# Reversed order within an attention step of a hybrid decoder layer on eight cores: value product, transposes, normalisation, then the scores of the newest unit

## The reference, cut to what matters

```python
s = jnp.einsum('nqkgd,nskd->nkgqs', q, k) * ATTN_SCALE      # 16 query heads, 4 key heads
s = jnp.where(mask, s, NEG)                                 # band of 128 keys
m = jnp.maximum(jnp.max(s, axis=-1, keepdims=True), sk)     # sk: the sink logit of the head
e = jnp.exp(s - m)
den = jnp.sum(e, axis=-1, keepdims=True) + jnp.exp(sk - m)
p = (e / den).astype(v.dtype)
o = jnp.einsum('nkgqs,nskd->nqkgd', p, v)
```

## Time and profile before

| | |
|---|---|
| three runs | 3579.36, 3603.8, 4138.53 us; median 3603.8 |
| the profiled execution | 3581.02 us |
| span of its slowest core, which the profile shows | 3579.5 us |
| spans of the eight cores | 3561.9 to 3579.5 us |
| mean granted TensorE clock of that core | 0.979 |
| busy: PE, DVE, ACT, POOL | 96%, 30%, 24%, 13% of the span |

### The profile page before, as it was taken

The page is one execution under the profiler, slowest core; times in us unless marked ns, Lnnn a source line. Parts: engine busy times, 40 slices in busy tenths (PEclk is TensorE's granted clock), DMA queues, the critical chain, the costliest instruction groups (busy, mean ns, idle before and its releaser), DMA issues.

```text
span 3579.5 us, 62299 instructions; the slowest of 8 cores (3561.9 to 3579.5 us)
## 1 busy us (share of the span) xinstructions
PE 3422.9 (96%) x24208; PEld 2206.9 (62%) x24208; DVE 1076.8 (30%) x2012; ACT 846.2 (24%) x1925; POOL 478.4 (13%) x604
## 2 busy tenths in 40 slices
PE   7979999999999989999999999998879999999997
PEld 5546777777776545666666666664546666666664
DVE  2424222222234435122222222345442222222223
ACT  2444122111101444113210201013441132110103
POOL 0112021011012113003000100121130030000003
PEclk9989999999999999999999999999989999999998
DMA  8774686677678373556555555676665676665663
GB/s 171 120 144 99 132 168 119 126 144 150 141 163 185 78 143 79 125 112 139 110 121 131 122 126 116 135 145 145 133 146 114 124 147 121 128 121 104 115 114 93
DMA packets 83264, 460.62 MB, mean 129 GB/s; under 512 B 7552, under 2 KB 39936, under 8 KB 61568
## 3 DMA queue, kind: packets, MB, share of 16 engines
q0 software_dynamic: 27520, 351.48, 53.0%
q1 hardware_dynamic: 55456, 105.17, 10.2%
HBM read 784.43 MB, written 31.49 MB: 228 GB/s over the span
## 4 chain that ended last, share of the span: by engine, by line
PE 86%; DVE 4%; DMA 4%; ACT 3%; issue 2%; POOL 1%; SPq 0%; DVEq 0%; ACTq 0%; POOLq 0%
PE ps L130 86%; DVE R L130 2%; DMA AT<-wdb 2%; ACT AT L130 1%; DVE TMP L130 1%; DMA yT<-R 1%; ACT TMP L130 1%; DMA MIX<-xm 1%; POOL R L130 1%; DVE sm L130 0%; ACT R L130 0%; DVE AT L130 0%; ACT ring L130 0%; SPq L130 0%; ACT GT L130 0%
## 5 line engine op out<-in xcount | busy, mean ns | idle before, releaser
L130 PE MATMUL ps<-N,w 128*128 128x384 bf16 (+3 forms) x11712 | 1796.1, 315 | 0.0
L130 PEld LDWEIGHTS ps<-N,w 128*128 128x128 bf16 x11712 | 1143.4, 98 | 643.5 <-issue 40.8
L130 PE MATMUL ps<-MIX,w 128*128 128x320 bf16 (+2 forms) x4608 | 688.8, 313 | 0.0
L130 PEld LDWEIGHTS ps<-MIX,w 128*128 128x128 bf16 x4608 | 450.9, 98 | 236.5
L130 PE MATMUL ps<-GT,w 128*128 128x320 bf16 (+2 forms) x3072 | 459.4, 313 | 0.0
L130 DVE SCALAR_TENSOR_TENSOR ring<-ps,TMP 128x320 f32<-128x320 f32 (+2 forms) x384 | 201.1, 524 | 678.6 <-PE ps L130 675.6
L130 DVE TENSOR_TENSOR R<-ps,R 128x320 f32<-128x320 f32 (+2 forms) x384 | 201.5, 525 | 676.4 <-PE ps L130 676.4
L130 PEld LDWEIGHTS ps<-GT,w 128*128 128x128 bf16 x3072 | 300.6, 98 | 157.9 <-issue 0.2
L130 PE MATMUL ps<-R,w 128*128 128x320 bf16 (+2 forms) x1536 | 247.4, 324 | 23.1 <-DVE R L130 11.9
L130 POOL TENSOR_TENSOR TMP<-TMP 128x320 f32<-128x320 f32 (+2 forms) x222 | 209.4, 947 | 432.9 <-ACT TMP L130 432.9
L130 ACT ACTIVATE TMP<-R 128x320 f32<-128x320 f32 (+2 forms) x288 | 138.7, 490 | 403.8 <-DVE R L130 394.0
(11 more groups left out here) (107 smaller groups left out, 1442.4 us busy)
## 6 DMA issues: line engine op xcount, KB each, us to landing
w<-w_up POOLq DMA_DIRECT2D x48, 2048.0 KB, 15.1
w<-w_dn POOLq DMA_DIRECT2D x48, 2048.0 KB, 14.4
w<-w_in POOLq DMA_DIRECT2D x45, 2048.0 KB, 14.3
w<-w_ac POOLq DMA_DIRECT2D x12, 2048.0 KB, 15.4
w<-w_out POOLq DMA_DIRECT2D x12, 2048.0 KB, 14.3
AT<-xm SPq DMA_DIRECT2D x32, 384.0 KB, 8.6
AT<-xm SPq DMA_DIRECT2D x32, 352.0 KB, 7.0
MIX<-uscr SPq DMA_DIRECT2D x52, 167.0 KB, 6.1
```

Of the source, the lines that this page charges most:

```text
L130: ins = getattr(engobj, fn[0])(*fn[1], **fn[2])
```

## The change

The loop over the steps runs the same four parts in the opposite order. Nothing else differs: the same instructions on the same units, banks and tiles.

```diff
             for k in range(n + 4):
                 if G.SA and k in (2, 9):
                     make_qc(k > 2)
+                if 0 <= k - 4 < n:
+                    units[k - 4].V()
+                if 0 <= k - 3 < n:
+                    units[k - 3].Tr()
+                if 0 <= k - 1 < n:
+                    units[k - 1].N()
                 if k < n:
                     units[k].S()
-                if 0 <= k - 1 < n:
-                    units[k - 1].N()
-                if 0 <= k - 3 < n:
-                    units[k - 3].Tr()
-                if 0 <= k - 4 < n:
-                    units[k - 4].V()
                 yield
```

## The result

The changed kernel is slower: ratio 1.0335 to the kernel before, 95% interval 1.0238 to 1.0433. Its two runs that count took 3714.59 us, the profiled one, and 3703.33 us; runs in which a whole die had a lower granted clock, which come with either kernel, are left out throughout. The ratio is taken to the mean of three runs of the kernel before (3579.36, 3582.6 and 3603.8 us). The forecast was 3690 us, in 3630 to 3745.

What follows compares the result with a forecast made beforehand. The prediction took a 4.84 us ring through ACT and DVE, near TensorE's 4.36 us, to bound attention steps. Its terms made 418.6 us against 313.7, +105 us on 3581, stated as 3690 us, range 3630 to 3745.

Steps and rivals of the forecast that it cites:

- The ring through GpSimd: 60 attention steps: GpSimd's sink copy waits behind the previous unit's multiply; 6.31 us a step without tanh, 7.73 with.
- V and Tr on DVE: 24 tanh steps: the reciprocal waits behind the dense group's product and Tr's masking, making a step 7.73 us.
- the masking: DVE's masking of Tr ahead of the reciprocal in the 24 tanh steps, 0.57 us each.
- the output of V: Tanh stages: each fourth step DVE brings V's result out ahead of the masking, 0.57 us, 3.4 us in all.
- The sum: All 60 attention steps: 227.2 + 185.5 + 5.9 = 418.6 us against 313.7 us before, +105 us.
- the parts that were named and left out: Table load in each group's first step and added mask in group 1 lengthen a ring; some 6 us, not counted.
- the last step of each group is partly caught by the emptying steps: Each attention group's last step, 3 us, partly overlaps four emptying steps; not counted, 9 us in the lower bound.
- The clock: TensorE's clock drop in attention, 1.38 us: hidden under a 6.31 us ring, up to 2.2 us over in 12 steps.
- The rival that had the clock in the attention cost 40 us: TensorE's clock stays low in the attention, making TensorE the bound: +40 us, time 3726 us, chance 0.13.
- Mostly hidden: Attention steps: TensorE already sets them at 5.23 us, so the longer ring costs +30 us, 3611 us; chance 0.13.
- faster: Attention: V's bank emptied earlier and transposes ahead of the scores remove TensorE's waits; at best 3529 us, chance 0.02.

## Why the prediction was right

**The ring through GpSimd.** Right, and shown. It was worked out as 6.31 us and 7.73 us a step; the trace has 6.32 in `q_stage`, 6.39 in `ua_stage` and 7.77 in the plain tanh steps of group 2. N moved alone gives 105.4 us, taking most sink copies away takes 94 us back, and a second multiply lengthens these steps by the 1.18 us that it adds. There are 61 waits of 2.1 us on average where 60 of 1 to 3 us were forecast. One sentence on the rows is loose, without effect on the sum: only a start on another engine lies 0.1 us behind the end before it. On the same engine the next start comes before that end (the tanh at 1227.40, with the last read of a sum ending at 1227.50). The links were taken from start to start, so they hold.

**V and Tr on DVE.** Right in kind, a little high in size. A plain tanh step of group 2 takes 7.77 us in the changed order and 7.18 us with N alone, which is the masking, worked out as 0.57 us. Over all steps the two kernels differ by 13.6 us (432.7 and 419.1), where 13.7 us for the masking and 3.4 us for the output of V were worked out. By themselves, ahead of S but with N behind it, V and Tr cost 9.4 us in the steps by the medians and give 3 us back at the sample units.

**The sum.** Somewhat low: 418.6 us, measured 432.7. The 36 steps without tanh took 236.2 us where 227.2 were worked out, and the 24 with tanh 196.5 where it was 191.4. Half of the 14 us are the parts that were named and left out: the load of ACT's table takes 1.28 us in the first step of each group, and the added mask 0.8 us in four steps of group 1, together 7.0 us. The rest is in the 6.39 us of `ua_stage`, taken as 6.31, and in the tanh stages of groups 1 and 3, where steps with more dense groups or with the output of V reach 8 us and more; these I had counted too few.

**From the sum to the time.** +105 us stood for 124.6 us by the cores' medians. Of these 121.5 are the 60 steps, and 3.1 us is everything else in the kernel. The forecast's distance from them is thus 14.1 us of steps that came out longer, 2.5 us of a base that was read on the one core with the highest sum, and the 3.1 us. That the last step of each group is partly caught by the emptying steps shows at best once: from group 1's last COPY_PREDICATED to group 2's first it is 4.1 us shorter by the medians, but behind group 3's last one 4.0 us longer.

**The clock.** The drop was there and its price was not. The granted clock fell to 0.86 to 0.89 in the three stretches. In the step shown, TensorE had been idle for 2.93 us up to 1264.00; from 1267.0 to 1272.5 us it was granted 0.56, the lower of its two levels for most of that time, and its dense group takes 4.88 us. The next one, from 1275.07, takes 2.77 us. Yet both steps are 7.77 us long, and so is the third, at 7.76. ACT's writes to TMP waited for TensorE seven times in either kernel, 79.8 us before and 79.6 after. So the slower TensorE fits into the idle time that the ring leaves. Of its 61 us of longer busy time some belong to core 7's stretch from 1420 us, where they did cost time; on core 5, which has none, TensorE is busy 3463.4 us, 40 more than before. The rival that had the clock in the attention cost 40 us falls. The sentence of the Trainium skill ("TensorE: Matmul & The Clock Gate", What's actually happening) that the prediction quotes fits the trace so far as the granted clock was lower, 0.86 to 0.89, where TensorE idled more; that TensorE then becomes the bound, which the rival drew from it, did not come.

**Mostly hidden, and faster.** Both fell as argued: 6.3 us a step did not hide behind 5.2. V alone ahead of the scores did nothing for the time.

**What it does not explain.** Cores 6 and 7 lost 17 us each to a granted clock of 0.83 from 1420 us on, behind the attention. The kernel before with two multiplies has a stretch like it on cores 2 and 3. No run tells what sets it off, and whether the changed attention makes it likelier stays open.

## What to carry to other kernels

In a software pipeline over engines with in-order queues, find for each step the ring that leads from a unit back to the next one, and add up its links; its length against the busiest engine's work says what a change of order may cost. An order that puts the old unit's work first costs time where an instruction of the new unit then stands behind it on its queue and comes later than the engine that waits for it can bear: here a copy of four columns, 0.19 us and harmless in one place, drew a whole multiply and a reciprocal into the ring. Slack is read from such a ring as well, and not from an engine's idle time: GpSimd was idle for 3.3 us of a step and had 0.7 to 1.1 us to spare in its plain steps. And the ring is also where a gain lies: moving the exponentials behind the next unit's scores (and N with them one unit later) took 1.5% off, with no work removed.

## What the runs showed of the hardware

In these rows a hand-off from one engine's end to another's start takes about 0.1 us between ACT and DVE and from POOL to ACT (1273.09 to 1273.18), but 0.2 us from DVE's reciprocal to GpSimd (1271.71 to 1271.92). Behind the start of a multiply of 1.04 us on GpSimd the small copy started 0.98 us later, and a second multiply 1.18 to 1.19 us later. The granted clock of TensorE was 0.86 to 0.89 after 0.93 to 0.96 in stretches that the ring through the other engines bounds, and steps with a dense group of 4.88 us were as long there as steps with one of 2.77 us.
